# A two-layer transformer with routed experts on one core: expert weights read as 16 KB per partition, and four buffers for gathered rows

## The reference

```python
for layer in range(DEPTH):                                   # DEPTH = 2
    mod = c_act @ ada_w[layer] + ada_b[layer]
    sh_a, sc_a, g_a, sh_f, sc_f, g_f = jnp.split(mod, 6, axis=-1)
    h = modulate(rmsnorm(x, norm_attn[layer]), sh_a, sc_a)
    y = diff_attention(...) if layer < 1 else dilated_attention(...)
    x = x + g_a * y
    h = modulate(rmsnorm(x, norm_ffn[layer]), sh_f, sc_f)
    x = x + g_f * hier_moe(h, ...)

def expert_block(args):                                      # in hier_moe, for rows of one expert
    xb, e = args
    return (jax.nn.silu(xb @ w_gate[e]) * (xb @ w_up[e])) @ w_down[e]
```

## Time and profile before

| | |
|---|---|
| time, median of 3 runs | 1898.48 us (1897.32 to 1899.91) |
| the profiled execution's own time | 1904.66 us |
| its span, first to last instruction | 1902.9 us |
| PE busy | 1518.0 us (80% of the span) |
| DVE, ACT, POOL busy | 514.1, 371.6, 91.6 us |
| transfers | 548.02 MB, 183413 packets, mean 288 GB/s |
| granted TensorE clock, mean | 0.900 of full speed |

### The profile page before, as it was taken

One profiled execution on the slowest core, in us unless ns is written; L12 is line 12 of the kernel. 1 busy time (PEld: TensorE's weight loads), 2 busy tenths in 40 slices (PEclk: granted clock), 3 DMA queues, 4 the chain that ended last, 5 costly groups with the idle time before them and its releaser, 6 DMA issues.

```text
span 1902.9 us, 16563 instructions
## 1 busy us (share of the span) xinstructions
PE 1518.0 (80%) x6360; PEld 671.8 (35%) x6360; DVE 514.1 (27%) x1178; ACT 371.6 (20%) x916; POOL 91.6 (5%) x99
## 2 busy tenths in 40 slices
PE   5999998997867757683698999998887756847845
PEld 2455554443222222231344455543432212312311
DVE  2675554340000000010576122225500100100103
ACT  3133344311101100110310234342210100101100
POOL 1000001010000000000000000002000000000000
PEclk9999998999878888897799999999998978978977
DMA  9972523389999999999766021021599999999996
GB/s 346 360 283 76 190 89 136 127 320 382 410 410 401 408 410 392 404 410 400 262 221 221 0 85 48 26 108 56 223 409 409 410 409 409 410 404 404 410 404 236
DMA packets 183413, 548.02 MB, mean 288 GB/s; under 512 B 8940, under 2 KB 46301, under 8 KB 182302
## 3 DMA queue, kind: packets, MB, share of 16 engines
q1 hardware_dynamic: 153536, 492.85, 66.5%
q0 software_dynamic: 12384, 36.41, 5.0%
q10 hardware_dynamic: 17406, 17.59, 2.9%
HBM read 530.37 MB, written 28.34 MB: 294 GB/s over the span
## 4 chain that ended last, share of the span: by engine, by line
PE 55%; DMA 27%; SPq 10%; DVE 5%; issue 2%; ACT 1%; DVEq 0%
PE psum L2144 12%; DMA ring<-in_moe_w_up_dram 11%; SPq L449 9%; PE psum L1897 9%; PE psum L1695 9%; DMA ring<-in_moe_w_down_dram 7%; PE psum L2177 5%; DMA ring<-in_moe_w_gate_dram 5%; PE psum L1867 3%; PE psum L1750 3%; DVE W L1080 1%; DMA T<-in_moe_w_up_dram 1%; DMA XN<-in_moe_w_up_dram 1%; DMA ring<-in_ada_w_dram 1%; PE psum L1724 1%
## 5 line engine op out<-in xcount | busy, mean ns | idle before, releaser
L2144 PE MATMUL psum<-ring,V 128*32 128x512 f32 (+2 forms) x1712 | 440.1, 677 | 182.1 <-DMA ring<-in_moe_w_up_dram 77.5
L2144 PEld LDWEIGHTS psum<-ring,V 128*32 128x32 f32 (+2 forms) x1712 | 145.2, 146 | 415.0 <-issue 408.5
L2177 PE MATMUL psum<-ring,V 128*32 128x512 f32 (+2 forms) x768 | 199.4, 661 | 74.0 <-DMA ring<-in_moe_w_down_dram 52.9
L975 ACT ACTIVATE V<-psum,modall,scls 128x128 f32<-128x128 f32 x216 | 81.3, 457 | 499.8 <-PE psum L2122 499.8
L1080 DVE SCALAR_TENSOR_TENSOR W<-ring,cact,W 128x512 f32<-128x512 f32 (+1 forms) x224 | 138.5, 618 | 7.7
L2144 PE MATMUL psum<-XN,V 128*32 128x512 f32 (+1 forms) x208 | 112.0, 700 | 23.0 <-DMA ring<-in_moe_w_gate_dram 15.2
L1494 DVE TENSOR_TENSOR V<-V,psum 128x512 f32<-128x512 f32 x28 | 19.3, 688 | 403.7 <-PE psum L2144 403.7
L2177 PEld LDWEIGHTS psum<-ring,V 128*32 128x32 f32 (+2 forms) x768 | 61.1, 141 | 168.8 <-issue 168.8
L1695 PE MATMUL psum<-HT,ring 128*128 128x512 f32 x256 | 115.4, 597 | 0.0
L2177 PE MATMUL psum<-XN,V 128*32 128x512 f32 (+2 forms) x192 | 101.4, 680 | 13.0 <-DMA ring<-in_moe_w_down_dram 13.0
L1510 DVE SCALAR_TENSOR_TENSOR HT<-psum,slot_gate,W 128x512 f32<-128x512 f32 x56 | 42.1, 751 | 255.1 <-PE psum L2177 255.1
(11 more groups left out here) (311 smaller groups left out, 1656.8 us busy)
## 6 DMA issues: line engine op xcount, KB each, us to landing
ring<-in_moe_w_up_dram SPq DMA_DIRECT2D x54, 2048.0 KB, 24.2
ring<-in_moe_w_gate_dram SPq DMA_DIRECT2D x53, 2048.0 KB, 23.5
ring<-in_moe_w_down_dram SPq DMA_DIRECT2D x48, 2048.0 KB, 22.9
ring<-in_ada_w_dram SPq DMA_DIRECT2D x16, 2048.0 KB, 15.6
XN<-in_moe_w_down_dram SPq DMA_DIRECT2D x12, 2048.0 KB, 22.9
ring<-in_ada_w_dram ACTq DMA_DIRECT2D x16, 1024.0 KB, 5.3
XN<-in_moe_w_gate_dram SPq DMA_DIRECT2D x7, 2048.0 KB, 25.8
XN<-in_moe_w_up_dram SPq DMA_DIRECT2D x6, 2048.0 KB, 19.3
```

What stands on the lines that cost most here:

```text
L975: ins = act.activation(V[:, 2 * D + b * D + k * P:2 * D + b * D + (k + 1) * P], bank[0][:, q * P:(q + 1) * P], ACT.Identity, bias=mod[:, 2 ...
L2144: ins = pe.matmul(bank[2 + 2 * i + b][half * w:(half + 1) * w, :], V[:, col:col + w], slot3(x)[:, k, :], start=(k == 0), stop=(k == KC - 1))
L2177: ins = pe.matmul(bank[6 + hf][half * w:(half + 1) * w, :], V[:, col:col + w], slot3(x, 4)[:, k, hf * HALF:(hf + 1) * HALF], start=(k == 0 ...
```

## The change

It does three things.

1. Each expert matrix is read as one contiguous piece of 16 KB per partition: partition p gets rows 8p to 8p+7 of gate and up and rows 4p to 4p+3 of down. Turned rows then hold features 8q to 8q+7, and hidden rows 4q to 4q+3.
2. What must match that order: `normalised` reads at a step of 32 bytes (`eights`); the silu and the product after it read PSUM at a step of 16 bytes (`by_fours`); the modulation vectors are written eight columns to 64 partitions (layer 0, `ffn_block`) or to 32 partitions (layer 1, `ffn_half`), which takes eight products in place of four or two; the router's weights come in two transfers in place of four.
3. Gathered rows have four buffers, `GATHERED = 4`: two in `V`, two in the upper half of `HT`. Four gathers are issued at the start of an expert stage, and then that for step p+4 when the rows of step p have been turned.

```diff
+GATHERED = 4
...
+        def ffn_block(i):
+
+            return slice(64 * (i % 2), 64 * (i % 2) + 64), 24 + KC * ((i - 6) // 2), KC * ((i - 6) // 2)
+
+        def ffn_half(i):
+
+            return slice(32 * (i % 4), 32 * (i % 4) + 32), 88 + KC * ((i - 4) // 4), KC * (3 + (i - 4) // 4)
...
         def expert_weights(l, e):
-            g = t["moe_w_gate"][l, ds(e, 1)].rearrange("o (a p j) n -> p (o a) (j n)", p=P, j=2)
-            u = t["moe_w_up"][l, ds(e, 1)].rearrange("o (a p j) n -> p (o a) (j n)", p=P, j=2)
-            d = t["moe_w_down"][l, ds(e, 1)].rearrange("o (k p) n -> p (o k) n", p=P)
+            g = t["moe_w_gate"][l, ds(e, 1)].rearrange("o (p j) n -> p (o j n)", j=KC)
+            u = t["moe_w_up"][l, ds(e, 1)].rearrange("o (p j) n -> p (o j n)", j=KC)
+            d = t["moe_w_down"][l, ds(e, 1)].rearrange("o (p j) n -> p (o j n)", j=4)
             return g, u, d
+
+        def by_fours(a):
+            return a.rearrange("p (q j) -> p j q", j=4)
+
+        def four(a):
+            return a.rearrange("p (j q) -> p j q", j=4)
...
+        def gathered(p):
+
+            b = p % GATHERED
+            return V[:, b * D:(b + 1) * D] if b < 2 else HT[:, b * D:(b + 1) * D]
...
+                    slot_free(m + i)
+                    sp.dma_start(slot(m + i), {"g": g, "u": u, "d": d}[kind]).then_inc(w_in[SLOT[m + i]], 16)
                     if kind == "d":
-                        load(m + i, d, k=4)
                         del expert[r]
-                    else:
-                        load(m + i, g if kind == "g" else u, k=4)
...
-                for p in range(2):
+                for p in range(GATHERED):
                     gather(tok[:, column(p)], p, s["gath"][p].sem)
                 pool.wait_ge(*s["flag_ready"](1))
 
                 for p in range(NB):
                     b = p % 2
-                    if p + 2 < NB:
+                    if p + GATHERED < NB:
                         pool.wait_ge(*s["xr_pe"](p * 2 + 2))
-                        gather(tok[:, column(p + 2)], b, s["gath"][b].sem)
+                        gather(tok[:, column(p + GATHERED)], p, s["gath"][p % GATHERED].sem)
...
-                    if pairs:
-                        to, x = to.rearrange("p (a j q) -> p a j q", j=2, q=P), x.rearrange("p (a q j) -> p a j q", j=2, q=P)
+                    if eights:
+                        to, x = to.rearrange("p (j q) -> p j q", j=KC), x.rearrange("p (q j) -> p j q", j=KC)
...
-                    at = V[:, 4 * D + b * HALF:4 * D + (b + 1) * HALF]
-                    dve.tensor_tensor(at, at, bank[4 + b][:, :], ALU.mult).then_inc(s["hid"].sem, 1)
+                    at = four(V[:, 4 * D + b * HALF:4 * D + (b + 1) * HALF])
+                    dve.tensor_tensor(at, at, by_fours(bank[4 + b]), ALU.mult).then_inc(s["hid"].sem, 1)
...
+                if 6 <= i < 10:
+                    rows, at, _ = ffn_block(i)
+                    for j in range(KC):
+                        ins = pe.matmul(bank[6][rows, at + j:at + j + 1], acc[:, j::KC], ones[:, 0:1], start=True, stop=True)
...
+                            if 4 <= i < 12:
+                                rows, at, _ = ffn_half(i)
+                                for j in range(KC):
+                                    ins = pe.matmul(bank[6][rows, at + j:at + j + 1], HALF_ACC[i % 4][:, j::KC], ones[:, 0:1],
+                                                    start=True, stop=True)
```

More of the change, by code:

```diff
@@ L308, in program @@
             y_evac=2 * NB, last_oh=1, row_add=TC, add_pe=2 * TC, x_new=TC)
-        turns = dict(gath=[16 * ((NB + 1) // 2), 16 * (NB // 2)], scat=[16 * (NB // 2), 16 * ((NB - 1) // 2)])
+        gath = [16 * len(range(i, NB, GATHERED)) for i in range(GATHERED)]
+        turns = dict(scat=[16 * (NB // 2), 16 * ((NB - 1) // 2)])
         sems = {n: sem(n) for n in counts}
-        sems2 = {n: [sem(f"{n}{i}") for i in range(2)] for n in turns}
+        sems2 = {n: [sem(f"{n}{i}") for i in range(len(k))] for n, k in turns.items()}
         rows_in = [sem(f"rows_in{c}") for c in range(TC)]
@@ L364, in program @@
               for l in range(LAYERS)]
+        gath_in = [(sem("gath_in0"), 0), (sem("gath_in1"), 0), (fb_out, 16), (hank_in, 16)]
+        for l in range(LAYERS):
+            sm[l]["gath"] = [Signal(x, used + l * gath[i]) for i, (x, used) in enumerate(gath_in)]
         ov_from_one = ["dn_pe", "xr_pe", "xr_t"]
@@ L623, in _, with gather @@
                 last_token, last_row = pool.to_reg(S - 1), pool.to_reg(2 * S - 1)
-                def gather(rows, b, signal):
-                    pool.indirect_dma_start(V[:, b * D:(b + 1) * D], None, xn_d[l],
+                def gather(rows, p, signal):
+                    pool.indirect_dma_start(gathered(p), None, xn_d[l],
                                             bass.IndirectOffsetOnAxis(ap=rows, axis=0),
@@ L1011, in _ @@
                             act.wait_ge(*o["gu_pe"](e * 2 + (2 * u0 + 1)))
-                            act.activation(V[:, 4 * D:4 * D + HALF], bank[2][:, :], ACT.Silu).then_inc(o["silu"].sem, 1)
+                            act.activation(four(V[:, 4 * D:4 * D + HALF]), by_fours(bank[2]), ACT.Silu).then_inc(o["silu"].sem, 1)
         @block.vector
@@ L1621, in mod_reduce @@
                 pe.wait_ge(mod_col, i)
-                for j in range(4):
-                    by_two = slice(2 * P * (j // 2) + j % 2, 2 * P * (j // 2 + 1), 2)
-                    ins = pe.matmul(bank[6][:, 4 * i + j:4 * i + j + 1], acc[:, by_two if 6 <= i < 10 else slice(j * P, (j + 1) * P)],
-                                    C[:, C_32:C_32 + 1] if i < 4 else ones[:, 0:1], start=True, stop=True)
+                if 6 <= i < 10:
+                    rows, at, _ = ffn_block(i)
+                    for j in range(KC):
+                        ins = pe.matmul(bank[6][rows, at + j:at + j + 1], acc[:, j::KC], ones[:, 0:1], start=True, stop=True)
+                else:
+                    for j in range(4):
+                        ins = pe.matmul(bank[6][:, 4 * i + j:4 * i + j + 1], acc[:, j * P:(j + 1) * P],
+                                        C[:, C_32:C_32 + 1] if i < 4 else ones[:, 0:1], start=True, stop=True)
                 ins.then_inc(mod_red, 1)
@@ L2121, in rows @@
                         k = 4 * r + q
-                        ins = pe.transpose(to[:, q * P:(q + 1) * P], V[:, b * D + k * P:b * D + (k + 1) * P], ident)
+                        ins = pe.transpose(to[:, q * P:(q + 1) * P], gathered(p)[:, k * P:(k + 1) * P], ident)
                     ins.then_inc(s["xr_pe"].sem, 1)
```

65 lines of the change are left out of this document (34 added, 31 removed).

## The result

The changed kernel takes 1884.61 us, median of four runs (1881.18 to 1887.38), against 1899.2 for the kernel before beside it: ratio 0.9921, 95% interval 0.9899 to 0.9943. It is faster by 15 us, less than half of the 35 that I forecast, and inside the range. Of all the runs reported here one, of the kernel with two buffers, fell into a slow state (2481.41 us, at a granted clock of 0.587) and is left out of that kernel's numbers.

The account below looks back on a forecast made before the run. Transfers of 2 MB matrices were taken to bound the expert stages. -43.2 + 2.5 + 1.5 + 2 + 1.4 + 1 = -34.8 us, from the median 1898.5 to 1864 us; range 1847 to 1885.

Parts of the forecast that it names:

- What bounds the kernel: Expert stages of both layers: PE waits for data, so the arrival of 2 MB matrices sets the end; elsewhere PE leads.
- The larger pieces: Expert matrices: 24 packets less per engine at 10 ns save 0.24 us per matrix, 20.6 us in layer 0, 22.6 in layer 1.
- The slots: Four-expert steps: layer 0's seven slots still suffice, margin 3.0 to 2.3 us; 1.5 us off for layer 0, 1 for layer 1.
- The gathers: First gather of each layer, slowed by 16 KB packets beside it: +1.5 us in layer 0, hidden by PE's delay in layer 1.
- the buffers win nothing: Expert steps: the chain inside a step has no gather in it, so the extra gather buffers gain nothing themselves.
- The layout: Costs outside the plateaus or hidden: half blocks of layer 1 +2 us, blocks 6 to 9 of layer 0 +1.4, normalisation +1.
- The rival with the small costs at their upper ends: Reductions at +16.7 us and layer 0's holes wider by 5, giving 1882 us; chance 0.10.
- its 12.5 us for the half blocks: Layer 1's half blocks 4 to 11: +12.5 us if a narrow product cost as much as a wide one.
- The normalisation: Last of each layer, on PE's path, reading at 32 bytes: 0 to 0.8 us per layer, +1 taken for both.
- Silu and product: Experts' PSUM reads at 16 bytes, 688 ns: even doubled, hidden behind PE's 9.9 us of other products, so 0.

Follow-up runs that it names:

- the 1.98 us block at 16 bytes: Block 6 of the kernel before with wrong-column reductions at other steps, here four products of 128 columns at 16 bytes; whole run 8114.16 us.
- the kernel with its products in turn: The changed kernel with VectorE's last sum turning the operand and neighbouring products going to different array columns; 1871.10 us, ratio 0.9837.
- the wide products at 32 bytes: The changed kernel with two blocks or four half blocks reduced together by 8 products of 128 columns; 1880.29 us, ratio 0.9886.

## Why the prediction was right in kind and wrong in size

- *What bounds the kernel*: right. Cutting the same transfers into other packets, two transfers for each matrix in place of one, moved 30 us.
- *The larger pieces*: right in mechanism, slightly too large. On the two pages SP's queue took 66.5% of 16 engines over 1902.9 us and takes 64.5% over 1879.4: 53 us less, over 73,728 packets spread on 16 engines 11.5 ns each, where I had 10. A matrix went from 5.17 to 4.96 us in layer 0 (406 to 423 GB/s) and from 5.13 to 4.92 in layer 1 (409 to 426), 0.21 in place of 0.24. Forecast 43.2 us, 39.2 with the slots and the gather, which the stages hold too; measured 36 by the stages.
- *The slots*: no hole at every four-expert step, as forecast; in layer 0 the loss is in the 423 where layer 1 has 426, and from 780 to 790 us, a stretch that was full before, the rate is 335 GB/s.
- *The gathers*: 7.68 to 10.02 us, +2.3 against +1.5. That PE's delay would hide it in layer 1 was wrong: it is on the chain there, and PE waits up to 3.5 us for it. That the buffers win nothing was wrong for the waits: with two buffers PE waits 32.6 us in all for gathered rows, and 27.2 us where only down comes in 16 KB pieces, where it was 1.1 in the kernel before. In the time they win 2 us, which is not clear of nothing.
- *The layout* is **the step that failed**: "eight of 64 columns for four of 128, between 8 x 0.10 and 8 x 0.26 against 1.05, middle 1.4", and "two wide ones (0.52) become eight narrow ones (0.82)". I priced a narrow product by its width, from a row whose operand lies together, and set the 32-byte step aside, though the prediction itself named the Trainium skill's 16-byte lines and said that they would hold for these weight loads. Measured: 2.08 us a block, the upper end (+4.1 us against +1.4); in layer 1 the stage of the value projections is 89.8 us in place of 85.9 (+3.9 against +2). And a term was missing altogether, the clock: 3.4 us in layer 0, and most of the 5.9 us behind the value projections of layer 1. That the slow loads pull it down in layer 0 is argued, not shown: from 80 to 122 us the five kernels with these loads all have dips and the seven others have none, but the 1.98 us block at 16 bytes has none behind it, and in the value projections of layer 1, with reductions of 1.15 and 1.91 us, the changed kernel's clock stays at 1.00. Of the 20 us that the medians are short of the forecast, the kernel with its products in turn brings back 14. The rival with the small costs at their upper ends, 1882 us, came nearest, in part by luck: its 12.5 us for the half blocks were 3.9, and the clock, which it did not have, made up for part of them.
- *The normalisation*: the mean of its 16 is 953 ns against 757, and PE waits 2.3 and 1.2 us for it in layer 1 where it was 1.6 and 0.8, so +1.1 there: the upper end. Silu and product cost nothing: 688 ns as before.

Layer 1 ahead of its experts is still 4.4 us longer in the best kernel (452.4 us) than before (448.0). Its value projections take 2.9 us more (88.8), 1.7 of them in the one projection at the lower clock and 0.6 in longer waits for VectorE; the normalisation has 1.1. What is left is within what two profiles differ by.

## What to carry to other kernels

Before an operand's layout is changed to make transfers longer, list every engine that will read it at the new step, and price each read at its step; a weight load was the dear one here (1.05 us for four of 128 columns at 8 bytes, 1.98 at 16 and 32), and the last VectorE operation ahead of it could turn the data for little: PE waits 0.3 to 0.6 us for it ahead of three of the four blocks. Small products to different columns of the array should take turns. And a stage that is bound by transfers repays a forecast from packets fairly well (36 us of 39), but the stages that pay for it have to be measured just as closely, their clock too.

## What the hardware showed that I had not expected

- Eight products of 64 columns by one take from 0.65 to 2.08 us, by the step of their operand and the order in which they go to the array's columns.
- PE's clock fell to 1.2 GHz for parts of the windows behind the slow weight loads, although PE has no idle time there in the profile (10.00 of 10.00 us): 0.83 to 0.86 in two of the windows between 80 and 112 us in the changed kernel's two profiles, 0.88 from 92 to 102 us with the wide products at 32 bytes, and 1.00 throughout from 80 to 122 us in the seven kernels whose reductions take less. In layer 1 it also fell behind a wait of 1.64 us with short loads.
- An issue of SP's held it for 4.8 us (median) where the matrix went in 4 KB packets, and for 0.33 us where it went in 16 KB packets.
- The first gather of a stage, 512 KB in 4 KB packets, takes 10 us beside 16 KB packets (10.02 and 10.08 in the changed kernel) and 7 to 8 beside 4 KB ones.
